# Attention C of a two-block layer stack: score rows on halves and strips of the array, side work moved between output and transposition

## What is computed

```
q = (rmsnorm(cq, g_cq) @ w_cq_b).reshape(B, S, 8, 96)
kv = (rmsnorm(ckv, g_ckv) @ w_ckv_b).reshape(B, S, 8, 128)
k_nope, v_c = kv[..., :64], kv[..., 64:]
qc = rmsnorm(q, gq_c);  kc = rmsnorm(concat([k_nope, k_pe]), gk_c)
qc = concat([qc[..., :64], rotate(qc[..., 64:])]);  kc the same
oc = softmax(qc kc^T * 96**-0.5) v_c
o = concat([oc, od]) * silu(gate);  x = x + o @ w_out
```

## Time and profile before

| | us |
|---|---|
| three runs | 3854.77, 3858.34, 3859.18 (median 3858.34) |
| profiled execution | 3851.71 |
| its span | 3849.7 |
| PE busy in the span | 3699.4 (96%) |
| DVE, ACT, POOL busy | 1981.7 (51%), 1326.0 (34%), 1023.6 (27%) |
| mean granted clock of PE | 0.987 |
| chain that ended last | PE 82%, DVE 10%, ACT 4%, issue 2% |
| a weight load from issue to landing (list of DMA issues) | 3.8 |

### The profile page before, as it was taken

One profiled execution on the slowest core, in us unless ns is written; L12 is line 12 of the kernel. 1 busy time (PEld: TensorE's weight loads), 2 busy tenths in 40 slices (PEclk: granted clock), 3 DMA queues, 4 the chain that ended last, 5 costly groups with the idle time before them and its releaser, 6 DMA issues.

```text
span 3849.7 us, 51842 instructions
## 1 busy us (share of the span) xinstructions
PE 3699.4 (96%) x21561; PEld 2906.7 (76%) x21561; DVE 1981.7 (51%) x2505; ACT 1326.0 (34%) x1603; POOL 1023.6 (27%) x634
## 2 busy tenths in 40 slices
PE   8999999999999999999999999999999999999988
PEld 7778888878788887888888777666677566767767
DVE  8464455524652537333413556655743655456663
ACT  3343433322330112111201344455624666444440
POOL 4212222222233345666433311110022001111001
PEclk9999999999999999999999999999999999999999
DMA  4111111111125422222522211100121001111011
GB/s 147 34 53 47 49 50 45 50 44 47 55 80 183 148 88 66 82 82 83 202 82 73 79 44 48 39 17 9 53 72 48 14 13 27 31 26 25 17 57 67
DMA packets 283160, 238.56 MB, mean 62 GB/s; under 512 B 16976, under 2 KB 255728, under 8 KB 282928
## 3 DMA queue, kind: packets, MB, share of 16 engines
q1 hardware_dynamic: 262128, 166.04, 14.8%
q10 hardware_dynamic: 20800, 69.22, 5.1%
HBM read 181.81 MB, written 49.35 MB: 60 GB/s over the span
## 4 chain that ended last, share of the span: by engine, by line
PE 82%; DVE 10%; ACT 4%; issue 2%; POOL 0%; DMA 0%; ACTq 0%; SPq 0%; DVEq 0%; POOLq 0%
PE ps L401 19%; PE ps L418 18%; PE ps L451 15%; PE ps L902 9%; DVE AR L2474 3%; PE ps L1273 2%; DVE SM L3306 2%; PE ps L701 2%; DVE AR L2482 2%; PE ps L1284 1%; PE ps L1264 1%; PE ps L1295 1%; PE ps L348 1%; PE ps L503 1%; PE ps L1344 1%
## 5 line engine op out<-in xcount | busy, mean ns | idle before, releaser
L3439 POOL CAST WH<-WR 128x1024 fp32r<-128x1024 f32 (+2 forms) x231 | 242.8, 1051 | 2567.5 <-DMA WR<-in_w_in 820.8
L3441 POOL TENSOR_TENSOR WL<-WR,WH 128x1024 fp32r<-128x1024 f32 (+2 forms) x231 | 500.9, 2169 | 18.5
L2474 DVE TENSOR_TENSOR AR<-AR 128x512 f32<-128x512 f32 (+3 forms) x426 | 452.0, 1061 | 56.5 <-ACT AR L1822 38.1
L418 PE MATMUL ps<-ARR,WH 128*128 128x512 f32 x1472 | 366.0, 390 | 2.2 <-ACT ARR L1919 2.2
L418 PEld LDWEIGHTS ps<-ARR,WH 128*128 128x128 f32 x1472 | 277.1, 188 | 60.5 <-ACT ARR L1919 2.7
L401 PE MATMUL ps<-XH,WH 128*128 128x512 f32 (+2 forms) x1168 | 300.2, 400 | 3.9 <-DVE AR L2474 1.7
L401 PE MATMUL ps<-XH,WL 128*128 128x512 f32 (+2 forms) x1168 | 290.1, 391 | 0.0
L401 PE MATMUL ps<-XL,WH 128*128 128x512 f32 (+2 forms) x1168 | 288.7, 389 | 0.0
L401 PEld LDWEIGHTS ps<-XH,WH 128*128 128x128 f32 (+2 forms) x1168 | 216.4, 188 | 57.2 <-issue 7.1
L3306 DVE TENSOR_REDUCE SM<-ps 128x1 f32<-128x1024 f32 x128 | 156.7, 1224 | 194.6 <-PE ps L1273 113.5
L401 PEld LDWEIGHTS ps<-XH,WL 128*128 128x128 f32 (+2 forms) x1168 | 218.3, 187 | 49.0
(11 more groups left out here) (295 smaller groups left out, 6255.8 us busy)
## 6 DMA issues: line engine op xcount, KB each, us to landing
WR<-in_w_in SPq DMA_DIRECT2D x78, 512.0 KB, 3.8
gates<-AR ACTq DMA_DIRECT2D x54, 512.0 KB, 2.7
AR<-gates SPq DMA_DIRECT2D x54, 512.0 KB, 4.4
H<-spill ACTq DMA_DIRECT2D x32, 512.0 KB, 6.1
WR<-in_w_in_e SPq DMA_DIRECT2D x26, 512.0 KB, 3.8
spill<-H ACTq DMA_DIRECT2D x24, 512.0 KB, 2.7
WR<-in_w_ffn_in SPq DMA_DIRECT2D x24, 512.0 KB, 3.8
WR<-in_w_in_o SPq DMA_DIRECT2D x23, 512.0 KB, 3.8
```

Source lines behind the costliest of these rows:

```text
L418: mm = pe.matmul(pt[:, h * 512:h * 512 + 512], wp[:, w % 4, k, :], xp(k)[:, h * 512:h * 512 + 512], start=i == 0, stop=i == 3 * nk - 1)
L2474: return v.tensor_tensor(o, x, y, op)
L3439: pool.tensor_copy(hi, full).then_inc(s_whi, 1)
L3441: pool.tensor_tensor(lo, full, hi, ALU.subtract).then_inc(s_wsplit, 1)
```

## The change

**Score rows.** The 96 rows of a head's query and key are split into 64 and 32. An even head keeps its own 64 in rows 0 to 63 and the rotated 32 in rows 64 to 95, and a copy of these in 96 to 127; an odd head has the rotated 32 in rows 0 to 31, their copy in 32 to 63, and its own in 64 to 127. S is then four matmuls on halves of 64 rows (L1286), the two heads alternating, and four on strips of 32 rows (L1292) that add to them, each of the four on a strip of its own.

**Side steps.** In C, PE's yield moves from behind T to between O and T; ACT's and DVE's stay behind their part of T. One step of side work (head 2's query projection) is taken ahead of the first unit on PE, ACT and DVE. The gate projection `gc` moves from side step 2 to step 3.

**To this end** an odd head's query weights come in three DMAs, the first two of 32 columns with a wait on SP, and its projection has 128 columns; ACT copies the shared key rows twice per head; DVE adds once more in the rotation (`again`); constants and gains for odd heads are added, the shared key rows move to rows 96 to 127 of the tables' tiles, and C's tables load 96 rows.

```diff
@@ PE @@
+            def query_c(h):
+                if h % 2:
+                    gemm(("qc", h), (cols(wcq, h * 96 + 64, 32, nk=2), cols(wcq, h * 96, 64, nk=2)),
+                         rhs=lambda k: A(18 + k), nk=2)
+                else:
+                    gemm(("qc", h), cols(wcq, h * 96, 96, nk=2), rhs=lambda k: A(18 + k), m=96, nk=2)
+            def key_c(h):
+                gemm(("kc", h), cols(wckv, h * 128, 64, nk=1), rhs=lambda k: A(28), m=64, nk=1, at=h % 2 * 64)
...
-                gemm(("qc", h), cols(wcq, h * 96, 96, nk=2), rhs=lambda k: A(18 + k), m=96, nk=2)
-                yield
-                hq(("qc", h), "w96", 96)
+                query_c(h)
+                yield
+                hq(("qc", h), "w96_odd" if h % 2 else "w96", P if h % 2 else 96)
+                key_c(h)
+                yield
+                pe.wait_ge(s_kraw, h - 1)
+                hn(("kc", h), "w96_odd" if h % 2 else "w96", [A(22)], P if h % 2 else 96)
                 if h % 2 == 0 and p >= 2:
                     xgemm(("gc", p), cols(wio, OG + p * P))
-                gemm(("kc", h), cols(wckv, h * 128, 64, nk=1), rhs=lambda k: A(28), m=64, nk=1)
-                yield
-                pe.wait_ge(s_kraw, h - 1)
-                hn(("kc", h), "w96", [A(22)], 96)
                 yield
...
-                            for m in range(2):
-                                pt, n = opn(("S", b, m))
+                            two = [opn(("S", b, m)) for m in range(2)]
+                            for pt, n in two:
                                 pe.wait_ge(freed[n % 4], n // 4)
-                                for h in range(2):
-                                    mm = pe.matmul(pt[:, h * 512:h * 512 + 512], q(p, m)[0:96, rows],
-                                                   k(p, m)[0:96, h * 512:h * 512 + 512], start=True, stop=True)
-                                mm.then_inc(filled[n % 4], 1)
+                            for h in range(2):
+                                for m, (pt, n) in enumerate(two):
+                                    e = slice(m * 64, m * 64 + 64)
+                                    pe.matmul(pt[:, h * 512:h * 512 + 512], q(p, m)[e, rows],
+                                              k(p, m)[e, h * 512:h * 512 + 512], start=True, stop=False,
+                                              skip_group_check=True)
+                            for h in range(2):
+                                for m, (pt, n) in enumerate(two):
+                                    e = slice(64 - m * 64 + h * 32, 96 - m * 64 + h * 32)
+                                    mm = pe.matmul(pt[:, h * 512:h * 512 + 512], q(p, m)[e, rows],
+                                                   k(p, m)[e, h * 512:h * 512 + 512], start=False, stop=True,
+                                                   skip_group_check=True)
+                                    if h:
+                                        mm.then_inc(filled[n % 4], 1)
...
                         mm.then_inc(filled[n % 4], 1)
+                    if kind == "C":
+                        yield
                     if 1 <= s < nu + 1:
...
-                    yield
+                    if kind == "B":
+                        yield
...
-            weave(att_c(), itertools.chain(chain(4, *[prep_c(h) for h in range(2, 8)]), chain(8, prep_d(0))))
+            side = itertools.chain(chain(4, *[prep_c(h) for h in range(2, 8)]), chain(8, prep_d(0)))
+            next(side)
+            weave(att_c(), side)
@@ ACT, shared key rows of a head @@
-                act.activation(kt[64:96, :], A(9)[96:128, :], ACT.Copy).then_inc(s_act_step, 1)
-                act.wait_ge(s_act_step, tick(s_act_step))
-                act.activation(A(22)[64:96, :], A(8)[96:128, :], ACT.Square).then_inc(s_kraw, 1)
+                for g in (c, c + 32):
+                    act.activation(kt[g:g + 32, :], A(26)[96:128, :], ACT.Copy).then_inc(s_act_step, 1)
+                    act.wait_ge(s_act_step, tick(s_act_step))
+                act.activation(A(22)[c:c + 32, :], A(25)[96:128, :], ACT.Square).then_inc(s_kraw, 1)
@@ DVE, rotate @@
+                if again is not None:
+                    TT(x[again, :], x[rows, :], tmp[rows, :], ALU.add).then_inc(s_dve_step, 1)
+                    v.wait_ge(s_dve_step, tick(s_dve_step))
                 TT(x[rows, :], x[rows, :], tmp[rows, :], ALU.add).then_inc(s_rope_tmp, 1)
@@ SP, load @@
+                if isinstance(src, tuple) and m == P:
+                    for c in (0, 32):
+                        sp.dma_start(dst[:, 0:nk, c:c + 32], src[0]).then_inc(s_half_in, 16)
+                    sp.wait_ge(s_half_in, 16 * (dups[0] + 2))
+                    dups[0] += 2
+                    src, dst = src[1], dst[:, 0:nk, 64:P]
```

More of the change, by code:

```diff
@@ L54 @@
 CE = CEPS2 + 1
-CW = {n: CE + 8 + i * 70 for i, n in enumerate(["w64", "w96", "w128", "w256", "w1024", "weps"])}
+CW = {n: CE + 8 + i * 70 for i, n in enumerate(["w64", "w96", "w128", "w256", "w1024", "weps", "w96_odd"])}
 NCST = CE + 8 + len(CW) * 70
@@ L2092, in tables @@
             def tables(which):
-                act.dma_start(A(25), a["rope"][2 * which]).then_inc(s_tab_in, 16)
-                act.dma_start(A(26), a["rope"][2 * which + 1]).then_inc(s_tab_in, 16)
+                rows = slice(0, 96 if which == 1 else P)
+                act.dma_start(A(25)[rows, :], a["rope"][2 * which][rows, :]).then_inc(s_tab_in, 16)
+                act.dma_start(A(26)[rows, :], a["rope"][2 * which + 1][rows, :]).then_inc(s_tab_in, 16)
             def gate(name, dst):
@@ L2162, in prep_c0 @@
                 act.wait_ge(filled[bank(("kpe",))], turn(("kpe",)))
-                act.activation(A(8)[96:128, :], PS[bank(("kpe",))][0:32, :], ACT.Copy)\
+                act.activation(A(25)[96:128, :], PS[bank(("kpe",))][0:32, :], ACT.Copy)\
                     .then_inc(s_act_step, 1)
@@ L2220, in prep_c @@
                     gate(("gc", p), A(14 + p % 2))
[L2221 to L2228, removed]
-                act.activation(kt[64:96, :], A(9)[96:128, :], ACT.Copy).then_inc(s_act_step, 1)
-                act.wait_ge(s_act_step, tick(s_act_step))
-                act.activation(A(22)[64:96, :], A(8)[96:128, :], ACT.Square).then_inc(s_kraw, 1)
-                act.wait_ge(s_kraw, tick(s_kraw))
-                yield
-                root()
                 yield
@@ L3068, in _, with rotate @@
             turns = [0, 0]
-            def rotate(x, tmp, ndma, rows=slice(0, P), i=0):
+            def rotate(x, tmp, ndma, rows=slice(0, P), i=0, again=None):
                 turns[i] += 16 * ndma
@@ L3126, in prep_c @@
                 hq(RS[h % 4], 96 ** -0.5)
-                rotate(A(CQ[h % 4]), A(27), 2, slice(64, 96))
+                rotate(A(CQ[h % 4]), A(27), 2, *((slice(0, 32), 0, slice(32, 64)) if h % 2 else (slice(64, 96), 0, slice(96, P))))
                 yield
@@ L3130, in prep_c @@
                 yield
[L3131 removed]
+                kb(A(CK[h % 4]))
                 yield
@@ L3481, in constants @@
         cst[:min(n, P), CW[f"w{n}"] + 6:CW[f"w{n}"] + 8] = 1.0 / n
+    for r in (slice(0, 32), slice(64, P)):
+        cst[r, CW["w96_odd"] + 6:CW["w96_odd"] + 8] = 1.0 / 96
     cst[:, CW["weps"] + 6:CW["weps"] + 8] = EPS / 1024
@@ L3520, in constants @@
     table(0, "pB", [(b + o, 16, ang) for b in (0, 64) for o, ang in ((0, row), (32, col))])
-    table(1, "pC", [(64, 16, angles(t, 32, 10000.0))])
+    table(1, "pC", [(b, 16, angles(t, 32, 10000.0)) for b in (0, 64)])
     part = angles(t, 16, 500000.0)
@@ L3563, in pack @@
     put("gkc", g("gk_c_2")[0])
+    for k, n in (("gqc_odd", "gq_c_2"), ("gkc_odd", "gk_c_2")):
+        put(k, np.concatenate([g(n)[0][64:], g(n)[0][64:], g(n)[0][:64]]))
     put("gsub", g("g_sub_d_2")[0])
```

64 lines of the change are left out of this document (44 added, 20 removed).

## The result

Four runs of the changed kernel took 3966.43 to 3977.46 us, median 3973.11; the kernel before took 3854.77 to 3864.49 in the runs beside it, median 3858.76. The ratio is 1.0294, with a 95% interval of 1.0274 to 1.0314.

A forecast was written before the change was run, and what follows sets the result against it. PE was taken as the bound, busy 367.95 of 383 us in C's stage. Profiled execution 3851.7 plus 75 us of delays and 37 of lowered clock made 3963.7; with the median 6.6 above, 3970, range 3920 to 4010.

The forecast's parts named there:

- The score rows: S in attention C: halves 1.92 us plus strips 1.02 make 2.94 us, 0.59 less than before.
- The rival with strips one after the other: S in C: the array runs 32-row strips serially, some 2.6 us a step, 83 in all, time 4050; chance 0.06.
- The chain: Each C step: S, O, side work, T, ACT's two copies, ACT's side operations, then S; PE idle from T's end.
- query step with V: Odd head's query projection with V's transposition as side work: 15.6 us against 11.54, +4.1.
- key step: Squares' sums and key projection as side work in C: 14.5 us against 10.86, +3.6.
- norm and spreading: Odd head's two steps with key norm and its spreading: 11.6 and 9.9 us, +2.4 for the two.
- norm with gate: Even head's norm step in C, which takes over the gate projection: 23.3 us.
- the fast rival: Side tile in C is free by T's end, so PE stays packed; time about 3835, chance 0.05.
- put at nothing: ACT's extra copy per head in C, covered by S and its first maximum; 6 us for six heads if uncovered.
- The clock: PE in C's stage: 17 stalls of 3.6 to 4.8 us, each costing 2.2 us at half clock, +37 us.
- The rival in which the clock holds: C's stage: the stalls come but the clock does not fall; time 3933, chance 0.18.
- The sign "ahead of each S": PE's timeline in C shows idle time of 3.6 to 4.8 us before each S, ACT's side operation as releaser.

The follow-up runs named there:

- ACT's order: The changed kernel with ACT's yield in C moved between the exponentials and T's copies, following PE's new order; 3889.82 us, ratio 1.0077.
- tiles by hand: The changed kernel with C's PSUM tiles assigned by role and a step's second side job moved behind T; 3894.05 us, ratio 1.0086.
- the spread version: On tiles: rotation over three side steps, query's second rows by DMA, key copies, T's tiles and D's V moved; 3855.44 us, ratio 0.9989.
- the filled stalls: The changed kernel with four unused matmuls behind T in twelve steps that end in a long stall; 3959.80 us, ratio 1.0260.
- the two runs above: Changed kernel with side work back behind T, no step ahead: 3893.03 us; kernel before with only the three moves of order: 3922.31 us.

## Why the prediction was right

The forecast was 3970, the time 3973.11. The mechanism is the one forecast, and its large parts stand the test one by one; smaller misses, told below, in part cancel, so the last 3 us are luck.

*The score rows.* Predicted 2.94 us, measured 2.99: halves 1.92 as in B, strips 1.07 where A's block gave 1.02. The Trainium skill (TensorE: Matmul & The Clock Gate, "Measured speedup vs the span model") gives four row tiles 3.07 times the speed; four blocks of 0.86 (a quarter of the query projection's 3.44) in 1.07 us are 3.2 times, so the trace agrees within a few per cent. The rival with strips one after the other falls. (Its price was also summed low: four times 0.95 less 1.02 is 2.78 a step and 89 us in all, not 2.6 and 83.)

*The chain.* The prediction's reading of the kernel before leaves out small waits: the gap of 1.55 comes four times in the stage, not once or twice a head, and waits for exponentials stand ahead of T (5.6 us in all) and of the key norm (3.3). Its account of the change holds. Measured from S to S, with the score block taken at its full-clock 2.99: query step with V 16.2 (predicted 15.6), even query step 14.0 (13.75), key step 17.32 - 2.51 = 14.8 (14.5), norm and spreading 21.0 (21.5), norm with gate 23.6 (23.3), last step with V 12.3 (12.3). The two runs that mend it from either side, ACT's order and the tiles, show that the cause is the one named, and that the fast rival's condition was stated rightly: once the side tile is free in time, 79 to 84 of the 114 us go. They also show that this rival's price was wrong. It would have given not 3835 but some 3890, as the next wait (O for T's copies, or T for O's tile) takes the place of the first; only with that one spread does the time come to 3855. The added copies and the fourth rotation operation, put at nothing, stand behind one long wait of the change (2.8 us, the first key norm); with the tiles by hand they are among what T and the key norms wait for.

*The clock.* Predicted 37 us from 17 stalls, measured some 35 and 16 stalls. PE's busy time in the stage should have fallen from 373.71 by 17.3 (32 blocks of 0.54) and by 3.44 (head 2's projection, now ahead of the stage) to 353, and the spread version's 351.1 at 0.99 says so too; it is 388.28, so the clock costs 35. That is close by some luck: D's norm step has a stall more than was counted and head 2's two did not come, and the 16 blocks behind the stalls lose 1.9 us each rather than 2.2, some 30 in all, with the rest in two blocks behind shorter stalls and in slow transpositions. By stretches (us, PE busy, clock), the stall of the key step above, its score block, and O and side work:

```profile
3116.30:3121.85 5.55, 1.89 (x17) 1.68 (x16) 0.10 (x1) 4.18 (x4) 0.00 (x0) 0.86 0.13 24
3121.85:3127.35 5.50, 5.50 (x16) 1.75 (x16) 0.00 (x0) 0.00 (x0) 0.00 (x0) 0.53 0.15 24
3127.35:3133.00 5.65, 5.65 (x57) 4.07 (x53) 4.73 (x9) 2.59 (x4) 0.00 (x0) 1.00 0.01 1
```

All sixteen stalls of 3.66 us and more were followed by a slow score block; of nine between 2.3 and 2.9 only two were. The rival in which the clock holds fails here, and the filled stalls show that it is the idle time and not the strips. The sign "ahead of each S" was too wide: 16 of 32 have such a stall.

*What was off.* Idle time has grown by 95.7, and with the shorter work (-17.3 and -3.4) this makes 75.0; the sum had +70 for the stage and +5 ahead of it, where 4.8 were measured (3.3 from head 2's projection and 1.5 from the rest, against 1.9 and 3.1). Heads 3 to 7 take 55.4 us more at full clock where the sum had 52, of which 1.8 are the three query steps with V; head 2, D and the last steps take 19.6 against 18. These are sizes, not steps.

On the Trainium skill's warning (TensorEngine Tiling (Array Packing), "PSUM Bottleneck") that the copying out of PSUM may become the bottleneck: the runs agree in a narrower sense. It was never ACT's amount of work, which is the same in the run that gives back 84 us, but its place in ACT's order and the PSUM tile that waited for it.

## What to carry to other kernels

Where tiles go round in the order of opening, moving a job moves every later job to another tile: write down for each job whose tile it takes and what that tile's emptier does first, before moving it. A job that is moved ahead on the producing engine must be moved on the emptying engine too, or be given a tile that nothing opens soon; else it will be waited for behind work that was made after it. And a gap of some 4 us on PE cost a further 1.4 to 2.5 us here, in the score block behind it, so a change that opens gaps is dearer than its idle time.

## What was not expected

Score rows on halves and strips shorten PE's work by 17 us and by themselves lose 34 (ratio 1.0087). Both tiles are filled at the same moment, 2.99 us after S began, where one was full after about 1.75 before; the first maximum starts later, and with it the exponentials on which T's second tile and the side job wait. Filling both tiles together takes away the head start of the first. That reading covers the 27.5 us of added idle time, as far as the layout's added work is not in them; the other 23 us are the clock.

The clock's low stretches do not vanish one by one with the stalls: twelve filled stalls freed twelve score blocks, some 23 us by the blocks, and 13 us came through, because six other blocks lost 8.5 us; three of them, behind stalls of 2.4 to 2.5 us, had been at full clock after the change. Nor does the clock come back when the long stalls go: by the same reckoning (PE's busy time less what its work takes) it costs 18 us with ACT's side work first (371.14 against 353) and 15 with tiles by hand (368.24 against 353), 23 and 25 in the two runs above, and nothing only in the spread version. So shorter waits cost clock as well, and 35 us for 16 stalls is no price per stall to carry over. Why some blocks behind short waits are slow and others not is open; no run here tells it apart.
